# Down products held behind the next up unit, and partial products of latent tiles drawn ahead

## The reference, cut to what matters

```python
gate, up = jnp.split(h @ w_ffn_in, 2, axis=-1)
return (jax.nn.silu(gate) * up) @ w_ffn_out
```

```python
for j in range(CONV_W):
    acc = acc + up[:, j:j + L] * conv_w[j]
a, g = jnp.split(acc, 2, axis=-1)
return (jax.nn.silu(g) * a) @ w_down
```

## Time and profile before

| | us |
|---|---|
| median of 3 runs | 2524.96 (2518.44 to 2526.46) |
| profiled execution | 2526.85 |
| its span | 2525.1 |
| TensorE busy | 2372.2 (94%) |
| VectorE busy | 1600.2 (63%) |
| ScalarE busy | 974.1 (39%) |
| GpSimd busy | 321.1 (13%) |

### The profile page before, as it was taken

One profiled execution on the slowest core, in us unless ns is written; L12 is line 12 of the kernel. 1 busy time (PEld: TensorE's weight loads), 2 busy tenths in 40 slices (PEclk: granted clock), 3 DMA queues, 4 the chain that ended last, 5 costly groups with the idle time before them and its releaser, 6 DMA issues.

```text
span 2525.1 us, 33201 instructions
## 1 busy us (share of the span) xinstructions
PE 2372.2 (94%) x13210; PEld 1915.8 (76%) x13210; DVE 1600.2 (63%) x2718; ACT 974.1 (39%) x1800; POOL 321.1 (13%) x325
## 2 busy tenths in 40 slices
PE   6988998999999899899999999999998999999996
PEld 3866567888888778566778888888887677888875
DVE  3638686565657642677778775556474987765455
ACT  4326453322212522567352232322442774423322
POOL 0210101000012200000100313223111000101223
PEclk9999999999999999999999999999998999999998
DMA  6430015744434212111412342333122103432221
GB/s 253 136 104 1 26 59 175 250 154 150 164 137 157 102 42 77 51 49 43 150 63 84 101 150 77 110 115 133 43 76 76 35 22 130 150 106 95 92 92 50
DMA packets 79162, 257.59 MB, mean 102 GB/s; under 512 B 5664, under 2 KB 10400, under 8 KB 70560
## 3 DMA queue, kind: packets, MB, share of 16 engines
q1 hardware_dynamic: 65024, 205.01, 23.6%
q0 software_dynamic: 12688, 46.14, 5.3%
q10 hardware_dynamic: 1296, 4.30, 0.4%
HBM read 246.00 MB, written 9.44 MB: 101 GB/s over the span
## 4 chain that ended last, share of the span: by engine, by line
PE 70%; DVE 14%; ACT 7%; issue 4%; DMA 2%; POOL 1%; SPq 1%; POOLq 0%; ACTq 0%; DVEq 0%
PE PS L1087 9%; PE PS L1089 9%; PE PS L1088 9%; PE PS L1158 5%; PE PS L1159 5%; PE PS L1160 5%; PE PS L948 4%; PE PS L846 3%; PE PS L843 3%; PE PS L844 3%; PE PS L961 2%; ACT HT L2469 2%; PE PS L992 2%; DVE SM L1833 1%; PE PS L891 1%
## 5 line engine op out<-in xcount | busy, mean ns | idle before, releaser
L1087 PE MATMUL PS<-HH,WH 128*128 128x512 f32 (+1 forms) x1088 | 421.3, 387 | 9.2 <-DVE TMP L2155 4.6
L1088 PE MATMUL PS<-HL,WH 128*128 128x512 f32 (+1 forms) x1088 | 417.7, 384 | 0.0
L1089 PE MATMUL PS<-HH,WL 128*128 128x512 f32 (+1 forms) x1088 | 417.7, 384 | 0.0
L2307 ACT ACTIVATE WH<-STG 128x1024 fp32r<-128x1024 f32 (+1 forms) x204 | 198.9, 1022 | 293.3 <-PE PS L1160 250.3
L2007 DVE TENSOR_TENSOR WL<-STG,WH 128x1024 fp32r<-128x1024 f32 (+1 forms) x204 | 242.4, 1230 | 48.7 <-ACT WH L2307 48.7
L1158 PE MATMUL PS<-WH,AH 128*128 128x512 f32 x616 | 247.7, 402 | 13.8 <-DVE WL L2007 5.0
L1159 PE MATMUL PS<-WL,AH 128*128 128x512 f32 x616 | 245.5, 399 | 0.0
L1160 PE MATMUL PS<-WH,AL 128*128 128x512 f32 x616 | 244.9, 398 | 0.0
L1087 PEld LDWEIGHTS PS<-HH,WH 128*128 128x128 f32 x1088 | 205.2, 189 | 52.3 <-DVE TMP L2155 5.2
L1088 PEld LDWEIGHTS PS<-HL,WH 128*128 128x128 f32 x1088 | 205.4, 189 | 40.4 <-issue 1.0
L1089 PEld LDWEIGHTS PS<-HH,WL 128*128 128x128 f32 x1088 | 205.1, 189 | 40.5
(11 more groups left out here) (224 smaller groups left out, 4276.6 us busy)
## 6 DMA issues: line engine op xcount, KB each, us to landing
STG<-in_w_up SPq DMA_DIRECT2D x66, 1024.0 KB, 6.4
ADAW<-in_w_ada SPq DMA_DIRECT2D x96, 512.0 KB, 3.8
STG<-in_w_down SPq DMA_DIRECT2D x20, 1024.0 KB, 5.4
ADAW<-in_w_ada POOLq DMA_DIRECT2D x32, 512.0 KB, 4.0
STG<-in_w_ffn_out SPq DMA_DIRECT2D x10, 1024.0 KB, 7.0
STG<-in_ev_w_in SPq DMA_DIRECT2D x8, 1024.0 KB, 5.2
STG<-in_w_in SPq DMA_DIRECT2D x6, 1024.0 KB, 6.7
spill<-X POOLq DMA_DIRECT2D x10, 512.0 KB, 4.6
```

What stands on the lines that cost most here:

```text
L1087: e.matmul(out, h_, hh, start=c == 0, stop=False)
L1088: e.matmul(out, h_, hl, start=False, stop=False)
L1089: return e.matmul(out, l_, hh, start=False, stop=c == 7)
```

## The change

`ffn_plan` holds the down steps of the chunk before WIDE's last chunk (the two-unit chunk) back and puts them behind the first up step of the last chunk. The order there was up 16, up 17, down h0, down h1, up 18 to 21, down, down; it is now up 16, up 17, up 18, down h0, down h1, up 19 to 21, down, down. This holds for layers 0 and 2. Since unit 18's activations are now made while those of 16 and 17 are still wanted, the last chunk's AH and AL lie in the upper half of their buffers (`acts`), and their first write waits for the chunk before the two-unit one (`acts_free`). All engines and SP's loads follow the new list.

In layer 1 `ahead` is no longer empty: in each chunk but the last the first half does the products of all but the last unit for the four latent tiles in front, then the last unit tile by tile, then the context tiles with all units. In the last chunk the first half's products of the first three units for tiles 2, 3 and 4 come first. What `ahead` leaves out for the context group is `range(0 if gi else len(ahead), n)`.

```diff
 def ffn_plan(chunks):
-    plan = []
+
+    plan, held = [], []
     for g, us in enumerate(chunks):
-        plan += [("up", g, u) for u in us]
-        for h in range(2):
-            plan += [("down", g, h, c, min(4, us[-1] + 1 - c)) for c in range(us[0], us[-1] + 1, 4)]
+        ups = [("up", g, u) for u in us]
+        downs = [("down", g, h, c, min(4, us[-1] + 1 - c)) for h in range(2) for c in range(us[0], us[-1] + 1, 4)]
+        plan += ups[:1] + held + ups[1:]
+        held = downs if own_place(chunks, g + 1) else []
+        plan += [] if held else downs
     return plan
+
+
+def own_place(chunks, g):
+
+    return chunks is WIDE and g == len(WIDE) - 1
...
             T = len(tts) * P
-            out.append([self.ff[L][n][:, off:off + len(us) * T].rearrange("p (c t) -> p c t", c=len(us)) for n in ("AH", "AL")])
+            o = off + 4 * T * own_place(CHUNKS[L], CHUNKS[L].index(us))
+            out.append([self.ff[L][n][:, o:o + len(us) * T].rearrange("p (c t) -> p c t", c=len(us)) for n in ("AH", "AL")])
...
-                ahead = range(n - 1) if len(groups) == 1 and h == 0 and n == len(us) else range(0)
+                ahead = range(n - 1) if h == 0 and n == len(us) else range(0)
...
-                        m = down(pi, gi, tt, bs[tt], c, range(len(ahead), n), us)
+                        m = down(pi, gi, tt, bs[tt], c, range(0 if gi else len(ahead), n), us)
...
-                for tt in LAT[:3] if len(groups) == 1 else ():
+                for tt in LAT[:3]:
...
-    return k.ends(("wo", L)) if g == 0 else [k.pe_down((L, g - 1, 1, GROUPS[L][-1][1][-1]))]
+    return k.ends(("wo", L)) if g == 0 else [k.pe_down((L, g - 1 - own_place(CHUNKS[L], g), 1, GROUPS[L][-1][1][-1]))]
```

## The result

The changed kernel takes 2514.0 us (median of 10, 2503.03 to 2517.56), the kernel before 2523.6 beside it (10 runs, 2518.44 to 2528.79): 9.6 us less, ratio 0.9961, 95% interval 0.9950 to 0.9973. That is 6.8 to 12.6 us less, where 8.1 were forecast. The profiled execution took 2516.15, its span is 2514.4.

What follows compares the result with a forecast made beforehand. TensorE was taken to bound the kernel, with 70% of the span in the chain of waits. Layer 2 -5.0, layer 0 +1.0, layer 1's last chunk -4.1 and inner chunks 0 sum to -8.1 us: 2516.9, range 2511 to 2523.

Steps and rivals of the forecast that it cites:

- Layer 2, -5.0: Two-unit chunk: AL wait and low clock go, -6.15 us; a new 1.1 us stall on second-half weights comes.
- Layer 0, +1.0: Two-unit chunk: four accumulations ahead of WL make the second half's stall 2.4 us in place of 1.4.
- SP's moved load: Layer 0: second-half weights' load, issued at about 759.6 behind two ADAW loads and needed at 766, holds barely.
- Rival (a): Layer 0: the new 2.4 us stall halves the clock, losing 1.7 or 3.4 us; about 2519.5; chance 0.20.
- Layer 1's last chunk, -4.1: The weights stall and its low clock go; transposes for layer 2 move from 1858.2 to 1854.1; bounds -5.0 and -1.5.
- VectorE instead of TensorE sets the last microsecond: Layer 1's last chunk: TensorE reaches the transposes at 1853.2, but VectorE's fourth-tile norm holds them to 1854.1.
- Rival (b): Layer 1's end: VectorE bounds it more tightly, so only 1 us is won there; 2520; chance 0.14.
- Inner chunks, 0: Layer 1's other chunks: TensorE's waits stay and the new order gains nothing; bounds 0 and +2 us per chunk.
- rival (d): Layer 1's inner chunks: late banks stall the second half, 6 us a chunk in four chunks; 2541; chance 0.05.
- longer waits on L2107: Layer 1: growth of TensorE's waits on these products, 2.3 us before, would show the prediction wrong.
- Rival (c): More is won: layer 0's stall stays 1.4, layer 2's is hidden, layer 1 gives 5.0; 2513.9; chance 0.16.
- Rival (e): Layer 2: held products wait as long, 3.3 us idle stays, only low clock's 2.9 is won; 2519.0; chance 0.05.

Runs made afterwards that it cites:

- e3: Changed kernel with layer 1's old product order put back, so only the holds in layers 0 and 2 remain; 2520.16 us, ratio 0.9994 to the kernel before.
- e4: Changed kernel with layer 0's old step order, so only layer 2's two-unit chunk is held; 2512.06 us, ratio 0.9965 to the kernel before.
- e1: Kernel before with layer 1's new product order alone, inner chunks and last chunk, nothing held; 2514.24 us, ratio 0.9977 to the kernel before.
- e2: Kernel before with the new product order in layer 1's last chunk alone; 2517.28 us in one run.
- e7: e6 with the weights of layer 2's held second half split before AH and AL of unit 18; 2509.56 us, ratio 0.9948 to the kernel before.
- e5: Changed kernel without a background conditioning step at layer 0's up 18, later steps sliding back; 2522.92 us, ratio 1.0011 to the kernel before.
- e6: Changed kernel with layer 0's background steps moved from up 18 to the held second half's down step; 2508.29 us, ratio 0.9931 to the kernel before.
- e8: Changed kernel with two latent tiles ahead, not three, in layer 1's last chunk; 2518.42 us in one run.
- e10: Changed kernel measured once more, unaltered; 2506.22 us, ratio 0.9941 to the kernel before.

## Why the prediction was right, and where its working was off

**The sum.** -8.1 forecast, -9.6 measured. The local terms, from profiles, sum to -8.5, or -6.9 where layer 0's clock falls. The interval of 6.8 to 12.6 holds both. That the time came so near is in part luck: the second measurement of the same kernel (10.8 to 18.9 less) holds neither the forecast nor the local sum, and its 2506.2 lies below the range of 2511 to 2523. What is over goes with the granted clock, 0.977 and 0.980 on average against 0.974 before, in stretches of the same code; why these executions were granted more is open. The forecast stands on its local terms, which the profiles bear out, and not on the time.

**Layer 2, -5.0; measured -4.8.** Right in mechanism and size. AL's wait and the low clock behind it went together: e3 shows it without layer 1's edits, e4 without the hold in layer 0, and e1 and e2, which do not hold, keep both. The new stall, measured from starts, was 1.3 against 1.1 (the row gives 1.11 idle): VectorE's first half of WL ends 6.8 us behind the last up start as worked out, and the matmul starts 0.15 behind that. e7 shows the cause. The clock did not fall behind it in any of the seven profiles that have it (changed, e3, e4, e5, e6, e8, e10).

**Layer 0, +1.0; measured +1.1, and +1.6 for the clock in this execution.** The four accumulations in front of WL were the right rows: 8.1 us from last up start to second half, as forecast (772.2 - 764.15). SP's moved load was in time. e4 takes the cost away by not holding, e6 by moving the accumulations. Rival (a), given 0.20, is what the profiled execution did; of four profiles with this stall (changed, e3, e8, e10) the clock fell in two, changed and e8. So few profiles speak for a chance nearer a half than a fifth, no more.

**Layer 1's last chunk, -4.1; measured -4.8.** The step that failed is "VectorE instead of TensorE sets the last microsecond". TensorE came to the transposes as worked out, 29.95 us behind the first down matmul (30.0 forecast). Its wait there was mis-sized: 0.9 us were forecast, 0.25 measured. The fourth tile's norm ended 30.41 us behind the first down matmul (1851.81) and not 30.9: VectorE came to its second tile 0.2 us earlier, and its pace per tile was 1840.14 - 1834.98 = 5.16 us, not 5.24. And only every fourth transpose needs the fourth tile: the first three began at 1851.35, 1851.46 and 1851.57, the fourth at 1851.86, and the 32 took 3.66 us where they take 3.4 unhindered. So VectorE sets a quarter of a microsecond; e8 shows that the rest is TensorE's, since a delay of 1.46 us there moves the end by 1.2. Rival (b), built on the same idea with a higher price, is excluded by the 4.8.

**Inner chunks, 0; measured 0** (e2), within the 1.0 us by which the stage differs between profiles. No stall of several microseconds was added in a chunk: rival (d) did not happen. One of the signs that I had named for being wrong, longer waits on L2107, did show (2.9 us in the changed kernel, 4.4 in e1, 2.3 before); it was a poor sign, since e2 has 3.7 with the old order. What I had not seen is the wait on AL of e2, which the new order can take away; it did not shorten the stage.

**Rival (c)**, layer 0's stall unchanged and layer 2's hidden, is not what the change does, but e7 shows that both can be had with two more edits. **Rival (e)** is excluded: no wait on AL is left at the held chunk, and the stall there is 1.11 us and not 3.11.

## What to carry to other kernels

Before work is held behind a cover, list what the engine that feeds it does in program order between the end of the cover and the next operand: here the old wait went, and the split queued behind AL and the background accumulations made the new one. A background step that is taken away must be put back early enough for its consumer: leaving one out, so that all later ones slid back (e5), lost all of the gain, while taking it two steps later (e6) kept it. And price a stall with the clock behind it: 3.3 us lost standing still in layer 2 cost 6.2 in the kernel before and in e2, and 4.9 in e1, where the low clock was shorter (3.4 us and not 6.8).

## What the runs showed of the hardware

Equal idle times of 2.28 us, at the same place of the same program, were followed by the low clock in two profiles of four; the 1.2 us there in the kernel before, e1, e2 and e4 never, 3.1 us in layer 2 in all three profiles that have it (before, e1, e2). In layer 1's first chunk 2.5 us of idle time, behind up matmuls of 256 columns, were followed by it in all nine profiles that have them. The Trainium skill (TensorE: Matmul & The Clock Gate, "Why this matters for your kernels") would let the shorter ones pass; the measurements at 2.28 us differ from it in two of four, those at 2.5 us in nine of nine.

VectorE's four accumulations of 128x1024 (two inputs from SBUF) took 4.87 us alone and 7.97 beside GpSimd's additions, 1.6 times as long (e6). Three of the four took 2.31 us each in place of 1.28, and GpSimd's additions beside them about 2.3 in place of 1.29; VectorE's products just before (L2118, one input from PSUM) kept their 0.68 us beside such an addition. The Trainium skill (GPSIMD Engine Reference, "1. Specifications") says that GpSimd shares its SBUF interfaces with VectorE, and names instructions with two SBUF inputs as those that collide; the trace agrees.

The same program's feed-forward part of layer 0 took 390.0 to 396.4 us in three profiles of identical code there (before, e1, e2), and 386.1 to 386.6 with the low clock taken out; one low-clock stretch of 3.4 us, 18 to 20 us into layer 2's part where all kernels are the same, stands in six of the twelve profiles; the medians of one kernel in two sessions were 9.6 and 16.7 us below before. A change of 1 to 3 us is to be read from stage lengths, not from the time.
